# Products of the norm issued one step ahead or just in time, and the last turned tiles taken out one tile sooner

## The reference, cut to what matters

```
def rmsnorm_2(x, g):
    x32 = x.astype(jnp.float32)
    y = x32 * lax.rsqrt(jnp.mean(x32 * x32, axis=-1, keepdims=True) + EPS)
    return y.astype(x.dtype) * g
# layer 2, with a shift and a scale computed from c:
#   h4 = rmsnorm_2(x, attn_norm_g) * (1 + scale) + shift   ->  @ w_in   (256 x 2048 @ 2048 x 1856)
#   h6 = rmsnorm_2(x, mlp_norm_g)  * (1 + scale) + shift   ->  @ w_ff1  (256 x 2048 @ 2048 x 8192)
```

## Time and profile before

| what | value |
|---|---|
| median of 3 executions | 2170.51 us (2169.32 to 2174.05) |
| the profiled execution's own time | 2174.05 us |
| its span, first to last instruction | 2171.7 us |
| TensorE busy | 2135.2 us, 98% of the span |
| VectorE, ScalarE busy | 1496.9 us (69%), 1060.8 us (49%) |
| mean granted TensorE clock | 0.995 of full speed |
| the h4 place of the change | about 1193 to 1219 us in the span |
| the h6 place of the change | about 1455 to 1481 us in the span |

### The profile page before, as it was taken

The page is one execution under the profiler, slowest core; times in us unless marked ns, Lnnn a source line. Parts: engine busy times, 40 slices in busy tenths (PEclk is TensorE's granted clock), DMA queues, the critical chain, the costliest instruction groups (busy, mean ns, idle before and its releaser), DMA issues.

```text
span 2171.7 us, 29423 instructions
## 1 busy us (share of the span) xinstructions
PE 2135.2 (98%) x11502; PEld 1844.9 (85%) x11502; DVE 1496.9 (69%) x1910; ACT 1060.8 (49%) x1525; POOL 48.2 (2%) x48
## 2 busy tenths in 40 slices
PE   9999999999999999999999999999999999999998
PEld 7888888888888888888878898888888888888886
DVE  5867775788798787888955666567654566556655
ACT  6654555554444444444444766555443444334443
POOL 3200000000000000000000100000000000000000
PEclk9999999999999999999999999999999999999999
DMA  8786434778798897887955524346555555555553
GB/s 301 271 298 245 153 127 160 260 297 322 273 335 305 292 350 276 333 303 288 345 195 172 206 88 155 136 166 226 190 194 194 193 194 190 193 192 183 192 183 128
DMA packets 73096, 494.46 MB, mean 228 GB/s; under 512 B 8458, under 2 KB 8634, under 8 KB 16768
## 3 DMA queue, kind: packets, MB, share of 16 engines
q1 hardware_dynamic: 69984, 480.54, 61.3%
q0 software_dynamic: 2400, 11.39, 1.5%
q10 hardware_dynamic: 576, 0.67, 0.1%
HBM read 490.40 MB, written 2.16 MB: 227 GB/s over the span
## 4 chain that ended last, share of the span: by engine, by line
PE 83%; ACT 5%; DVE 5%; DMA 4%; issue 2%; POOL 0%; DVEq 0%; SPq 0%; ACTq 0%
PE region L1019 38%; PE region L963 25%; PE region L967 13%; DMA m_RAW<-in_ffn_w_in 3%; ACT m_WHI L1384 2%; PE bank L1052 2%; PE bank L1089 1%; DVE m_WLO L1725 1%; DMA m_RAW<-in_ffn_w_out 1%; PE region L1008 1%; DVE m_ACC L1778 1%; PE bank L1002 1%; PE bank L1061 1%; ACT m_SP L1478 1%; PE bank L1205 1%
## 5 line engine op out<-in xcount | busy, mean ns | idle before, releaser
L1725 DVE TENSOR_TENSOR m_WLO<-m_RAW,m_WHI 128x1024 fp32r<-128x1024 f32 (+3 forms) x732 | 877.1, 1212 | 530.2 <-ACT m_WHI L1384 511.3
L1384 ACT ACTIVATE m_WHI<-m_RAW 128x1024 fp32r<-128x1024 f32 (+3 forms) x732 | 753.6, 1040 | 731.4 <-PE region L1019 359.6
L1019 PE MATMUL region<-m_WHI,m_HL 128*128 128x512 f32 x1152 | 364.2, 397 | 0.8 <-DVE m_HL L1913 0.5
L963 PE MATMUL region<-m_HL,m_WHI 128*128 128x512 f32 x1472 | 359.5, 394 | 1.7 <-DVE m_kcT L1663 1.7
L963 PE MATMUL region<-m_H,m_WHI 128*128 128x512 f32 x1376 | 329.7, 391 | 0.0
L963 PEld LDWEIGHTS region<-m_HL,m_WHI 128*128 128x128 f32 x1472 | 270.5, 189 | 54.0 <-DVE m_kcT L1663 2.0
L963 PEld LDWEIGHTS region<-m_H,m_WHI 128*128 128x128 f32 x1376 | 252.5, 188 | 48.7
L1019 PEld LDWEIGHTS region<-m_WHI,m_HL 128*128 128x128 f32 x1152 | 213.1, 189 | 42.8 <-issue 1.3
L1019 PE MATMUL region<-m_WLO,m_HL 128*128 128x512 f32 x576 | 225.7, 392 | 0.0
L1778 DVE SCALAR_TENSOR_TENSOR m_ACC<-m_RAW,m_cact,m_ACC 128x2048 f32<-128x2048 f32 x90 | 211.1, 2345 | 3.3 <-DMA m_RAW<-in_w_mod 3.3
L1019 PE MATMUL region<-m_WHI,m_HIDH 128*128 128x512 f32 x512 | 199.2, 389 | 0.0
(11 more groups left out here) (302 smaller groups left out, 1862.4 us busy)
## 6 DMA issues: line engine op xcount, KB each, us to landing
m_RAW<-in_w_ff SPq DMA_DIRECT2D x124, 1024.0 KB, 4.8
m_RAW<-in_w_mod SPq DMA_DIRECT2D x96, 1024.0 KB, 6.1
m_RAW<-in_ffn_w_in SPq DMA_DIRECT2D x88, 1024.0 KB, 6.1
m_RAW<-in_ffn_w_out SPq DMA_DIRECT2D x44, 1024.0 KB, 7.4
m_RAW<-in_nsa_w_in SPq DMA_DIRECT2D x36, 1024.0 KB, 5.0
m_RAW<-in_nsa_w_out SPq DMA_DIRECT2D x16, 1024.0 KB, 4.9
m_RAW<-in_w_out SPq DMA_DIRECT2D x16, 1024.0 KB, 4.8
m_RAW<-in_w_in SPq DMA_DIRECT2D x6, 1024.0 KB, 7.2
```

The lines of the kernel that those rows point to most:

```text
L963: mm = e.matmul(region[s["reg"]][:, b, :], hi[:, i, c:c + 128], both[:, k + a + i, :, :].rearrange("p a s -> p (a s)"), start=k + a + i == ...
L1019: mm = e.matmul(o, lhs, rhs, start=start and i == 0, stop=fin and i == 2, skip_group_check=True)
L1384: e.activation(WHI[u % 4][:, 0:(z - a) * ncol], raw[:, a * ncol:z * ncol], ACT.Copy).then_inc(a_hi, 1)
L1725: e.tensor_tensor(WLO[u % 4][:, 0:m], raw[:, a * ncol:z * ncol], WHI[u % 4][:, 0:m].bitcast(F32), ALU.subtract).then_inc(v_lo, 1)
```

## The change

It issues each product in the norm entry of its own first tile, so P(m) stands in entry m for m = 0, 1, 2, 4, 6, 8, 10, 12, 14. It also puts the turnout entry behind the eighth norm entry instead of the ninth. Buffers, waits and the amount of work stay the same, and it works alike on h4 and h6. One line fewer shifts the later line numbers by one: line 2019 is 2018 after it.

```
-                if normed[x] == 9:
+                if normed[x] == 8:
                     put("turnout", x, 12)
...
-                if m == 2:
-                    low(1)
-
-                first, n = {0: (0, 1), 1: (1, 1), 2: (2, 2), 3: (4, 2)}.get(m, (m + 2, 2 if m % 2 == 0 and m + 2 < KT else 0))
-                if n:
+                if m == 1 or m % 2 == 0:
+                    n = 1 if m < 2 else 2
                     r = 2 if x == "h4" else 3
                     root = by_token(rstd, n)
+                    if m == 2:
+                        low(1)
...
-                    e.tensor_tensor(HT[first % 8 // 4][:, first % 4:first % 4 + n, :], XGT[:, first:first + n, :], root,
+                    e.tensor_tensor(HT[m % 8 // 4][:, m % 4:m % 4 + n, :], XGT[:, m:m + n, :], root,
                                     ALU.mult).then_inc(v_ht, 1)
                 if m > 0 and m != 2:
                     low(m - 1)
```

More of the change, by code:

```diff
@@ L2014, in vector_program @@
                         w.wait_ge(b_out[6], filled(("rowcast", r), 6))
[L2015 to L2018, removed]
-                    e.tensor_tensor(HT[first % 8 // 4][:, first % 4:first % 4 + n, :], XGT[:, first:first + n, :], root,
+                    w.wait_ge(b_out[4 + m % 4 // 2], filled(("xturn", x, m // 4 * 4), 4 + m % 4 // 2))
+                    if m >= 8:
+                        w.wait_ge(a_norm, base + m - 6)
+                        w.wait_ge(v_norm, base + m - 6)
+                    e.tensor_tensor(HT[m % 8 // 4][:, m % 4:m % 4 + n, :], XGT[:, m:m + n, :], root,
                                     ALU.mult).then_inc(v_ht, 1)
```

## The result

The changed kernel takes 2184.91 us (median of 4 runs, 2184.34 to 2186.60), the kernel before on the same chip 2169.91 (4 runs, 2169.00 to 2174.05). The two medians are 15.0 us apart; the ratio on record is 1.0063, with a 95% interval of 1.0049 to 1.0077, which is 13.7 us slower, 10.6 to 16.7. The forecast was 2182.1, in 2177 to 2187, and slower.

The account below looks back on a forecast made before the run. TensorE, busy 2135.2 of 2171.7 us, was taken as the bound. Losses 5.36 + 4.86 = 10.2, plus 1.35 for the clock, gave 11.6; the profiled 2174.05 became 2185.6, less 3.54 for the median: 2182.1, range 2177 to 2187.

Parts of the forecast that it names:

- h4, waits in the stage: At h4, added TensorE waits make the stage end at 1224.27 instead of 1218.91: 5.36 us lost.
- h6, waits in the stage: At h6, same entries without final pairs, tile 11 at 1476.61 instead of 1471.83: 4.86 us lost.
- clock: TensorE's clock may fall behind its long waits, 0 to 1.0 at h4, 0 to 1.7 at h6; one fall taken, 1.35.
- The ring: In both stages S, P, N, next H, next S take turns; ScalarE waits about 2 us for P(8), P(12), P(14).
- the walk: Step-by-step pass through the new order at h4 and h6 with start-to-start prices from the trace: 5.36 and 4.86 us lost.
- Waits of N in total: ScalarE's N waits for products, on top of each stage's first waits: 8.6 us at h4, 9.9 at h6.
- The turnout: Moving the turnout entry alone, with products in their old places, costs 0.5 us at h4.
- What lies behind: After h4, VectorE and ScalarE have reserve and GpSimd's later memsets cost nothing: 0 us.
- 0 to 1.0: Price range in us of a clock fall at h4, where the wait at tile 13 hides part.
- hidden: Rival: the change is hidden because VectorE is 69% busy over the span; 2170.5 us, chance 0.04.
- half absorbed: Rival: in both stages only the waits ahead of tile 7 stay, 4.2 up to about 5 us; 2175, chance 0.09.
- The low tiles come sooner: Rival: low tiles no longer queue behind later products on VectorE; 1.6 us gained, 2168.9, chance 0.03.

Follow-up runs that it names:

- finals later: Third and fourth pair of h4's final copies put behind ScalarE's evacuation of slab 0, against the filled kernel: 2180.15 us, ratio 1.0043.
- filled kernel: Changed kernel plus 5 and 8 constant matmuls on TensorE ahead of tiles 7 and 11 of slab 0 in both stages: 2182.68 us, ratio 1.0055.
- h4 alone: Both parts of the change made at h4 only, h6 as in the kernel before: 2176.84 us, ratio 1.0029.
- products alone: Changed kernel with the turnout back in its old place behind norm entry 8, so only the products move: 2183.1 us, ratio 1.0055.
- products one entry ahead: Kernel before with every product from P(4) on one entry ahead of its own instead of two, turnout in its old place: 2172.6 us, ratio 1.0013.

## Why the prediction was right, and where its sum was short

| term | forecast | measured | by which run |
|---|---|---|---|
| h4, waits in the stage | 5.36 | 5.7 | finals later: 31.39 − 25.66 |
| behind h4: next slab waits for the evacuation | 0 | 1.15 | filled kernel and h4 alone: 32.52 and 32.55, against 31.39 |
| h6, waits in the stage | 4.86 | 4.9 to 5.05 | filled 29.72, products alone 29.91, against 24.86 |
| clock | 1.35 (one fall of two) | 0 at h4, 1.4 to 1.6 at h6 | after: 31.30 at h6, against 29.91 and 29.72 |
| sum | 11.6 | 13.3 in the profiled stages; 13.7 (10.6 to 16.7) timed | |

- **The ring** is right, step by step: ScalarE waits 1.95 us ahead of N(8), N(12) and N(14) ("about 2"). Counted from the first product, S407 starts at 23.70 by the walk and at 23.99 in the trace, and tiles 7 and 11 are 0.12 and 0.25 off. Putting H ahead of N gives 11 us back, which no rival explains.
- **Waits of N in total**: 18.5 us more were forecast, 16.8 came (22.6 − 5.8).
- **The turnout**: 0.5 by the walk, 0.7 and 0.8 in the trace.
- **Waits in h4**: 5.73 (31.39 − 25.66) where the walk had 5.36. At tile 11 the stage is 0.25 behind the walk (21.33 against 21.08). From there to tile 15 a tile costs TensorE 0.707 us in the run with the finals later and 0.693 in the kernel before, which makes 0.16 for twelve tiles. Why it costs more at a granted clock of 1.00 is open.
- **"What lies behind" at nothing** is the step that failed. It looked at GpSimd's memsets, their first reader and a weight load, and not at who must empty the region of slab 0 so that the next slab can start. In the kernel before, this evacuation ended at 1217.05 + 0.69 = 1217.74, 1.17 us ahead of TensorE's need at 1218.91:

```profile
1217.05 0.69 DVE L1666 SCALAR_TENSOR_TENSOR m_qaT<-region,m_qaT 128x512 f32<-128x512 f32 x1 [1.16 <-ACT m_qaT L1323]
```

  In the changed order the late final pairs stand ahead of its ScalarE half, and TensorE waits 1.0 us for it. That the measured time still lies in the range is owed to the 2 to 3 us that the range allows for scatter; the sum did not have this term.
- **The clock**: the forecast took one fall of two at 1.35. In the profiled execution both came, behind the 2.17 us ahead of tile 11 at h4 and the 2.18 at h6. The two windows are the 4 us behind the start of tile 11 in each.

```profile
1209.34:1213.34 4.00, 4.00 (x14) 3.43 (x15) 1.82 (x3) 2.57 (x5) 0.00 (x0) 0.57 0.74 272
...
1478.58:1482.58 4.00, 4.00 (x14) 3.43 (x15) 2.86 (x5) 2.05 (x5) 0.00 (x0) 0.59 0.83 289
```

  At h6 that cost 1.4 to 1.6 us (31.30 against 29.91 and 29.72). One fall of two was a guess between cases, and that the two that came cost about what one was priced at is luck. At h4 it cost nothing: tile 15 came 0.6 later than in the run with h4 alone (31.30 against 30.69), but the next slab had to wait for the evacuation anyway (0.39 us instead of 0.99), so the stage ends at 32.55 in both. The range "0 to 1.0" held it at its lower end.
- **Rivals**: hidden, and half absorbed, fell with the result itself (13.7 us, 10.6 to 16.7, where they had 0 and about 5), and with the run with h4 alone, in which the stage's 6.9 us arrive at the end (+6.8 timed). "The low tiles come sooner" is true of one product out of nine (P(14)), and worth 0.75 us.

What stays open: how often each of the two falls comes in the changed kernel's timed runs, since only the profiled one shows its clock by place.

## What to carry to other kernels

When two engines hand small results to each other while both also prepare the next weight part, the work that the partner waits for belongs ahead of one's own long step; one entry of lead gave back most of the loss here. Price a moved instruction by what is queued behind its waiter on the waiter's engine, up to and past the end of the stage: there, ask who has to empty the buffer that the next stage writes. And check the releaser named for a wait against the end times: in the three waits of the changed kernel shown above it was another one each time, while in the run with products one entry ahead it was the right one.

## What the runs showed of the hardware

The same idle time of TensorE does not always bring the clock down from 2.4 to 1.2 GHz. Behind the wait of 2.17 us ahead of tile 11 the granted clock fell in two stages of five without fills (both of the changed kernel; in neither stage of the run with the products alone, and not in the run with h4 alone). Behind the wait of 2.78 us ahead of a latent slab (1316.78 in the kernel before) the 5 us that follow have a clock of 1.00 in two profiles of ten and 0.50 to 0.71 in eight, and behind the one of 1.80 us (1330.37) 1.00 in two of ten and 0.66 in eight. In two profiles (products alone, h4 alone) the fall began before the wait of 2.78 us had ended. The falls at these places last about 3.4 us each, but the one at 1319 in the run with the products alone is twice as long. The ten kernels are alike at these places, so falls can be a part of the scatter of several us between executions of one kernel; no run shows it for the timed executions.

The Trainium skill ("TensorE: Matmul & The Clock Gate", section "A second HAM failure mode: psum-queue depth-cycling") tells of a kernel in which frequent short idles between groups of matmuls made the clock swing. No run here shows that: in the run with products one entry ahead TensorE had four waits of up to 0.9 us for low tiles in each stage, with a granted clock of 1.00 in both; the falls in and behind the changed stages stood behind or within single waits of 1.8 us and more.
